# Stick-breaking attention heads: five sample sums, three gate blocks behind the triangles, masks followed bank by bank

## What is computed

```
z = einsum('bqhd,bkhd->bhqk', q, k) * SB_HEAD_DIM ** -0.5
mask = k_pos[None, :] < q_pos[:, None]
log_keep  = where(mask, log_sigmoid(-z), 0)
log_after = cumsum(log_keep, reverse over keys) - log_keep
w = where(mask, exp(log_sigmoid(z) + log_after), 0)
out = einsum('bhqk,bkhd->bqhd', w, v)
```

## Time and profile before

| what | value |
|---|---|
| time, three runs | 4937.35, 4944.21, 4944.24 us; median 4944.21 |
| span of the profiled execution | 4942.6 us (first to last instruction) |
| its own time | not listed apart from the three; the median is 1.6 us above its span |
| TensorE busy | 4694.3 us, 95% of the span |
| heads of attention | from about 67 to 606.7 us, DMA share 0.92, 330 GB/s |
| rest of the program behind them | 4335.9 us, DMA share 0.58 |

### The profile page before, as it was taken

How to read it: one execution, slowest core, us unless ns; L and a number is a source line. 1 busy time by engine, 2 the same in 40 slices (tenths; PEclk the granted TensorE clock), 3 DMA queues, 4 the chain that set the end, 5 groups by cost and what they waited for, 6 DMA issues and landing times. The chain is left out here.

```text
span 4942.6 us, 90862 instructions
## 1 busy us (share of the span) xinstructions
PE 4694.3 (95%) x35332; PEld 4499.6 (91%) x35332; DVE 2965.4 (60%) x4754; ACT 1393.2 (28%) x1798; POOL 2246.3 (45%) x865
## 2 busy tenths in 40 slices
PE   6999989999999898979999989999999999999997
PEld 6999888888888798979998989999999999999997
DVE  3333245555555432339986956655777777777777
ACT  3323322222222221122223333332322322322322
POOL 1222222212221133324443235555877877877876
PEclk8999999999999999989999999998999999999999
DMA  6999833333333277863333455546888888888884
GB/s 237 335 336 337 306 120 132 128 127 129 132 122 131 86 236 245 298 209 104 103 108 154 187 209 186 160 148 240 299 310 300 298 304 299 300 310 299 299 299 170
DMA packets 344271, 1078.94 MB, mean 218 GB/s; under 512 B 99456, under 2 KB 154112, under 8 KB 264960
## 3 DMA queue, kind: packets, MB, share of 16 engines
q1 hardware_dynamic: 292272, 784.66, 45.9%
q0 software_dynamic: 36864, 268.45, 14.5%
q10 hardware_dynamic: 14928, 22.84, 1.3%
HBM read 877.69 MB, written 198.14 MB: 218 GB/s over the span
## 5 line engine op out<-in xcount | busy, mean ns | idle before, releaser
L154 POOL TENSOR_TENSOR wlo<-raw,whi 128x2048 fp32r<-128x2048 f32 x174 | 801.9, 4609 | 2094.6 <-ACT whi L150 1797.9
L168 POOL TENSOR_TENSOR wlo<-raw,whi 128x1024 fp32r<-128x1024 f32 x424 | 1043.2, 2461 | 501.1 <-ACT whi L164 496.4
L164 ACT ACTIVATE whi<-raw 128x1024 fp32r<-128x1024 f32 x424 | 449.6, 1060 | 1012.6 <-PE psS L236 380.3
L236 PE MATMUL accs<-xh,whi 128*128 128x272 f32 x2624 | 577.7, 302 | 54.2 <-POOL wlo L154 26.4
L2234 DVE SCALAR_TENSOR_TENSOR Y<-R,HD,Y 128x2048 f32<-128x2048 f32 x127 | 441.4, 3475 | 233.7 <-DMA R<-in_v,IDX 229.3
L236 PE MATMUL accs<-xh,wlo 128*128 128x272 f32 x2624 | 546.6, 290 | 0.6 <-issue 0.5
L236 PE MATMUL accs<-xl,whi 128*128 128x272 f32 x2624 | 545.4, 289 | 0.0
L236 PE MATMUL accs<-hh,whi 128*128 128x272 f32 (+1 forms) x1696 | 465.1, 323 | 47.4 <-POOL wlo L154 23.1
L236 PEld LDWEIGHTS accs<-xh,whi 128*128 128x128 f32 x2624 | 415.2, 190 | 81.0 <-issue 35.6
L236 PE MATMUL psS<-hh,wlo 128*128 128x416 f32 x1344 | 475.1, 353 | 0.0
L236 PE MATMUL psS<-hh,whi 128*128 128x416 f32 x1344 | 472.2, 351 | 0.0
(11 more groups left out here) (398 smaller groups left out, 9638.4 us busy)
## 6 DMA issues: line engine op xcount, KB each, us to landing
raw<-in_u SPq DMA_DIRECT2D x128, 1024.0 KB, 4.9
raw<-in_v SPq DMA_DIRECT2D x128, 1024.0 KB, 5.7
raw<-in_w_in SPq DMA_DIRECT2D x82, 1024.0 KB, 8.3
at_UI<-in_u SPq DMA_DIRECT2D x64, 1024.0 KB, 9.0
u_d<-at_UO SPq DMA_DIRECT2D x256, 256.0 KB, 6.2
g_d<-STG SPq DMA_DIRECT2D x8, 3328.0 KB, 10.3
Ge<-g_d SPq DMA_DIRECT2D x64, 416.0 KB, 10.8
wo_UI<-in_u SPq DMA_DIRECT2D x24, 1024.0 KB, 8.7
```

The lines of the kernel that those rows point to most:

```text
L154: pool.tensor_tensor(self.lo[:, c % 2, :], self.raw[:, c % 2, :], self.hi[:, c % 2, :].bitcast(F32), ALU.subtract).then_inc(self.split_don ...
L164: act.activation(self.half(self.hi, c, h), self.half(self.raw, c, h), ACT.Copy).then_inc(self.hi_done, 1)
L168: pool.tensor_tensor(self.half(self.lo, c, h), self.half(self.raw, c, h), self.half(self.hi, c, h).bitcast(F32), ALU.subtract).then_inc(se ...
L236: mm = pe.matmul(out, w(k), x(k, n), start=a, stop=z)
```

## The change

The sample's sums take 5 products: one of 160 columns with the triangle, and for each key block b from 1 to 4 one product with the ones that adds it to all earlier blocks at once. Of the gate's 16 blocks 13 stay ahead of the triangles and 3 run behind them. The output products start with blocks 3 and 1 and wait for each mask apart. On ScalarE a small Exp (`at_warm`) loads the table early, and the Sigmoid with the split of weight 5 moves behind the three Exp. On VectorE six turns stand ahead of SPL and two behind the masks. The core of the diff:

```
-        UNITS = 4
+        UNITS, BEHIND = 4, 3
...
-                project(3)
+                pe.wait_ge(S["at_acc_free"], UNITS * i + 4)
+                gate = unit_product(pe, W, 3, acc[1], xh, xl, UNITS, i)
+                for _ in range(KB - BEHIND):
+                    next(gate)
...
-                for b in range(5):
-                    mm = tri(lambda _: zbank["B"][:, 256 + 32 * b:288 + 32 * b], range(b, 5), smp)
+                pe.matmul(zbank["B"][:, 256:416], cst["negtri"][:, :], SPL[:, ZS:ZS + 160], start=False, stop=False,
+                          skip_group_check=True)
+                for b in range(1, 5):
+                    mm = pe.matmul(zbank["B"][:, 256:256 + 32 * b].rearrange("p (c t) -> p c t", c=b), cst["negones"][:, :],
+                                   SPL[:, smp(b)].unsqueeze(1).to_broadcast([P, b, DEC]), start=False, stop=False,
+                                   skip_group_check=True)
                 mm.then_inc(S["tri_ready"], 1)
                 tri(lambda b: z_at(0, b * P), (0, 1, 2, 3), cols).then_inc(S["tri_ready"], 1)
-
+                for mm in gate:
+                    pass
+                mm.then_inc(W.used, 2)
...
-                pe.wait_ge(S["wt_ready"], 4 * i + 4)
...
+                pe.wait_ge(S["wt_ready"], 4 * i + 1)
+                for kb in (3, 1):
+                    outputs(kb)
+                pe.wait_ge(S["wt_ready"], 4 * i + 3)
+                outputs(2)
...
+                pe.wait_ge(S["wt_ready"], 4 * i + 4)
+                outputs(0).then_inc(S["at_o_ready"], 1)
...
-                W.wait_used(act, 3, UNITS, i)
...
-                W.split_hi(act, 5, UNITS, i)
+                act.activation(warm[:, :], warm[:, :], ACT.Exp, scale=0.0).then_inc(S["at_warmed"], 1)
+                act.wait_ge(S["at_warmed"], i + 1)
...
                     act.activation(WT[:, zcols[b]], zbank[b], ACT.Exp).then_inc(S["wt_exp"], 1)
+
+                W.wait_used(act, 3, UNITS, i)
+                act.wait_ge(S["gate_stored"], 16 * i + 16)
+                act.activation(GB[:, :].rearrange("p (h t) -> p h t", h=2), acc[1][:, :, 0:H2],
+                               ACT.Sigmoid).then_inc(S["at_acc_free"], 1)
+                W.split_hi(act, 5, UNITS, i)
...
-                for c in range(TURNS - 1):
+                for c in range(TURNS - 2):
                     R.turn(dve, c, i)
...
-                R.turn(dve, TURNS - 1, i)
-                dve.wait_ge(S["wt_exp"], 3 * i + 3)
...
+                for n, at, parts in ((1, ZCOL[3], 2 * P), (2, ZCOL[2], P), (2, ZS + 128, DEC), (3, ZCOL[0], P)):
+                    dve.wait_ge(S["wt_exp"], 3 * i + n)
...
+                for c in range(TURNS - 2, TURNS):
+                    R.turn(dve, c, i)
```

More of the change, by code:

```diff
@@ L458, in attention @@
         GB, OT = sb("GB", [P, T]), sb("OT", [P, T])
+        warm = sb("at_warm", [P, 1])
         UI, UO = sb("at_UI", [P, 2, D]), sb("at_UO", [P, 2, D])
@@ L531, in head @@
                     pe.wait_ge(S["at_cst"], 64)
-                    pe.wait_ge(S["pad_set"], 1)
+                    pe.wait_ge(S["pad_set"], 2)
                 pe.wait_ge(S["at_acc_free"], UNITS * i + 4)
@@ L567, in head, with outputs @@
                 tri(lambda b: z_at(2, b * P), (2, 3), cols)
-                for b in range(5):
-                    mm = tri(lambda _: zbank["B"][:, 256 + 32 * b:288 + 32 * b], range(b, 5), smp)
+                pe.matmul(zbank["B"][:, 256:416], cst["negtri"][:, :], SPL[:, ZS:ZS + 160], start=False, stop=False,
[4 more added lines that the diff above has]
+                                   skip_group_check=True)
                 mm.then_inc(S["tri_ready"], 1)
                 tri(lambda b: z_at(0, b * P), (0, 1, 2, 3), cols).then_inc(S["tri_ready"], 1)
-                pe.wait_ge(S["vtm_evac"], 2 * i + 2)
-                pe.wait_ge(S["wt_ready"], 4 * i + 4)
-                for kb in range(4):
-                    pe.matmul(psR[:, 1, kb * P:SEQ], VTM[:, kb, :], WT[:, cols(kb)], start=kb == 0, stop=kb == 3,
-                              skip_group_check=True)
+                for mm in gate:
+                    pass
+                mm.then_inc(W.used, 2)
+                def outputs(kb):
+                    return pe.matmul(psR[:, 1, kb * P:SEQ], VTM[:, kb, :], WT[:, cols(kb)], start=kb == 3, stop=kb == 0,
+                                     skip_group_check=True)
+                pe.wait_ge(S["vtm_evac"], 2 * i + 2)
+                pe.wait_ge(S["wt_ready"], 4 * i + 1)
[3 more added lines that the diff above has]
+                outputs(2)
                 for b in range(4):
                     pe.matmul(psS[:, 0, 0:DEC], CV[:, b, :], WT[:, smp(b)], start=b == 0, stop=False)
-                pe.matmul(psS[:, 0, 0:DEC], VTM[0:DEC, 4, :], WT[0:DEC, smp(4)], start=False,
-                          stop=True).then_inc(S["at_o_ready"], 1)
+                pe.matmul(psS[:, 0, 0:DEC], VTM[0:DEC, 4, :], WT[0:DEC, smp(4)], start=False, stop=True)
+                pe.wait_ge(S["wt_ready"], 4 * i + 4)
+                outputs(0).then_inc(S["at_o_ready"], 1)
             head(0, True)
@@ L592, in _ @@
             act.sem_inc(S["o_stored"], 16)
+            act.wait_ge(S["pad_set"], 2)
             with act.Fori(0, HEADS) as i:
@@ L627, in _ @@
                     act.activation(WT[:, zcols[b]], zbank[b], ACT.Exp).then_inc(S["wt_exp"], 1)
+                W.wait_used(act, 3, UNITS, i)
[3 more added lines that the diff above has]
+                W.split_hi(act, 5, UNITS, i)
+                act.wait_ge(S["at_acc_free"], UNITS * i + 6)
+                act.dma_start(gates_d[bass.ds(i, 1)].rearrange("a p n -> (a p) n"), GB[:, :]).then_inc(S["gate_stored"], 16)
                 act.wait_ge(S["at_o_ready"], i + 2)
@@ L642, in _ @@
             dve.memset(KT[:, T:SEQ + P], 0.0).then_inc(S["pad_set"], 1)
+            dve.memset(warm[:, :], 0.0).then_inc(S["pad_set"], 1)
             R.start(dve)
@@ L657, in _ @@
                 ch.end()
-                R.turn(dve, TURNS - 1, i)
-                dve.wait_ge(S["wt_exp"], 3 * i + 3)
-                n = 0
-                for at, parts in ((ZCOL[3], 2 * P), (ZCOL[2], P), (ZCOL[0], P), (ZS + 128, DEC)):
+                for n, at, parts in ((1, ZCOL[3], 2 * P), (2, ZCOL[2], P), (2, ZS + 128, DEC), (3, ZCOL[0], P)):
+                    dve.wait_ge(S["wt_exp"], 3 * i + n)
                     s = slice(at, at + parts)
```

## The result

The changed kernel takes **4984.12 us**, median of 4 runs (4982.93 to 4987.46), against 4943.6 (4 runs, 4937.35 to 4944.24): ratio 1.0085, interval 1.0072 to 1.0098. Slower by 0.85%; forecast 4990 in 4955 to 5010. Its profiled execution has a span of 4981.1 us and a time of 4982.93.

The account below looks back on a forecast made before the run. The prediction saw TensorE and transfers both near their limits, and late weight 4 setting the changed loop. Seven longer loops +47.6, head 0 -7.8, end stores +6 make +46 on 4942.6, so 4988.6; forecast 4990 us, range 4955 to 5010.

Parts of the forecast that it names:

- The loop through weight 4: Mask to mask: moved turns issue weight 4 one round later, ScalarE waits; 73.7 us against 66.9, +47.6 over seven loops.
- landing: Weight 4's load from issue until it has landed: 10.7 us in the loop.
- pace: SP queue, three rounds from a head's first store to the issue of weight 4: 40.5 us.
- The ends: Head 0 ends 7.8 us sooner; at attention's end the wait for the last two turns' stores costs 6 us.
- TensorE's clock: Triangles start at granted clock 0.50 after about 10 us idle; 2.6 us of the loop is slow clock.
- The recurrent branch that follows is otherwise untouched: Behind attention: no further change of time in the recurrent branch.
- TensorE's 5.9 us: Saving per head on TensorE: sample products 2.1, idle time filled by gate blocks 2.2, output products 1.6 us faster.
- GpSimd's part of weight 5 too, with nobody waiting for either sooner: GpSimd's part of weight 5 moves later with the Sigmoid and split, like the gate's store, and this costs nothing.
- transfers speed up: Rival: weight 4 lands in 5.5 us, rounds' loads in 7.1; 62 us a loop, 4908 us; chance 0.13.
- my two theories: Output products' slow clock: it falls behind the idle time ahead of them, or the fifteen narrow products set it off.

Follow-up runs that it names:

- e3: Changed kernel with weight 4's split moved on ScalarE from behind V's copy to behind the Ln: 4933.48 us, ratio 0.9982.
- e4: Changed kernel with weights 3, 4 and 5 loaded one round earlier in SP's list: 4939.07 us, ratio 0.9991.
- e12: Kernel before with ScalarE's new order alone (early Exp, Sigmoid and weight 5's split behind the three Exp), fifteen products: 4930.69 us, ratio 0.9978.
- e8: e1 with all 16 gate blocks ahead of the triangles and one wait for all four masks: 4899.34 us, ratio 0.9913.
- e1: Changed kernel with VectorE's turns back in their old places, everything else still changed: 4898.73 us, ratio 0.9907.
- e5: e1 with all 16 gate blocks ahead of the triangles, output products still following each mask: 4891.35 us, ratio 0.9895.
- e11: Kernel before with five sample products and ScalarE's new order, one wait for all masks: 4908.56 us, ratio 0.9931.
- e9: Kernel before with five sample products in place of fifteen, nothing else: 4945.61 us, ratio 1.0008.
- e7: e1 with one wait for all four masks, gate blocks still behind the triangles: 4892.30 us, ratio 0.9897.
- e2: Kernel before with VectorE's turns alone moved (six ahead of SPL, two behind the masks): 5022.70 us, ratio 1.0150.
- e10: Kernel before with VectorE masking each bank right behind its own Exp, nothing else: 4937.74 us, ratio 0.9991.
- e6: e1 with fifteen sample products of 32 columns in place of the five: 4922.63 us, ratio 0.9964.

## Why the prediction was right, and where it was not

**The loop through weight 4: right, term by term.** Head 1 against the forecast: last mask to first store 121.33 to 123.59, 2.3 (2.35); to the issue of weight 4 at 165.32, 41.7 (40.5); landing, to 176.67, 11.4 (10.7); to the end of the Ln at 184.60, 7.9 (7.9); to the first triangle, 2.9 (2.9); to the last mask at 196.79, 9.3 (9.3). Sum 75.5; the seven loops lie between 71.9 and 75.5, mean 73.7, the forecast's number. That it is hit to the tenth is luck: over the seven loops the mean pace is 41.1 (forecast 40.5), the landing 10.3 (10.7), split to Ln 8.1 (7.9), triangles to last mask 9.0 (9.3), and these misses cancel. That weight 4's is the last of several late loads is shown by e3 and e4, where the loop shrinks by 7.0 and 5.4 and the next one appears.

**The ends: right, one of them by luck.** Head 0 gave 8.5 (7.8), the stores at the end cost 6.3 (6). But the forecast's terms for the stores, 2.35 + 2 x 3.85 + 6.2, add up to 16.25 and not to 15; what was measured is 15.04, because the stores took longer to issue (9.29 us for the eight) and less to land (4.6 us, median). Attention +45.3 against +46.

**TensorE's clock: right.** It is 0.50 behind the wait for SPL, which is 6.2 to 8.1 us long (about 10 forecast); the part ahead of the sample's product took 4.42 us in head 1. In head 3, at full speed by then, the five products took 1.16 (336.68 to 337.84; 1.15 forecast).

**"The recurrent branch that follows is otherwise untouched": 5.4 us off.** From its first to its last weight load of KM (L887, after L908) it takes 918.9 us before and 913.5 after. That is most of the 6.8 us by which the span grows less than the attention, 38.5 against 45.3, and so of the difference between 4990 and 4984. Of the 5.4 us, 3.4 are TensorE's clock (below). That the change did this is not shown: it is one execution of each kernel.

**TensorE's 5.9 us: the amounts right, what brings them in part wrong.** One loop each of before, e12, e8 and e1, without a fall of the clock (length, then TensorE's busy time):

```profile
129.87:195.45 65.58, 63.37 (x475) 60.30 (x475) 22.59 (x22) 22.20 (x24) 18.33 (x4) 1.00 0.95 342
127.96:193.05 65.09, 63.35 (x475) 60.29 (x475) 21.88 (x21) 22.61 (x26) 18.45 (x4) 1.00 0.92 328
184.72:247.00 62.28, 61.17 (x455) 58.10 (x455) 22.16 (x21) 22.50 (x26) 18.45 (x4) 1.00 1.01 364
493.95:554.90 60.95, 60.95 (x457) 58.05 (x456) 22.28 (x21) 22.51 (x25) 18.45 (x4) 1.00 1.00 361
```

From before to e1 the busy time falls by 2.4 us, the idle time from 2.2 to nothing, and slow clock cost 66.9 - 65.6 = 1.3 us of a mean loop before; the forecast had 2.1, 2.2 and 1.6, and a path of 61.0 against 60.95. (The mean loop of e1 is 0.8 longer, mostly for the 4.3 us of waits for SPL in seven loops.) What the forecast had wrong is which edits remove the idle time. It gave all of it to the gate blocks, and nothing to ScalarE's order or to the masks followed apart. The idle time falls with ScalarE's order from 2.2 to 1.74 (e12), with masks apart on VectorE to 1.10 (e8), and to nothing with TensorE's waits apart (e5) or with the gate blocks (e7); either is enough. In mean loops, taken one upon the other: ScalarE's order 1.5, most of it clock (before to e12), five products 2.4 (to e11), masks apart on VectorE 0.6 (to e8), TensorE's waits apart 1.2 (to e5), gate blocks behind **-0.6** (to e1). The step that failed is "GpSimd's part of weight 5 too, with nobody waiting for either sooner": VectorE was held by it for 0.5 us, by a wait that no semaphore shows. The profile of before had the evidence: 1.40 against 0.93 us for the same four masks, in the rows that I divided by four.

**The rival "transfers speed up"** (62 a loop, 4908): its loop is that of e1. But in the changed kernel weight 4's landing stayed at 9.8 to 11.3 us in the seven heads, mean 10.2 (10.7 forecast), though the transfers' share in head 1 fell from 0.94 to 0.86. The 5.5 us that this rival took as the least seen come from a load issued at 608.49, behind the heads; of those issued between 60 and 600 us the least is 8.3, so the trace of before spoke against it more than the forecast said.

## What to carry to other kernels

A piece of filler work that is moved on one engine moves every queue that waits for it: follow the list of the queue, find the critical load behind it, and price it with that load's own place in the list. Two chains that end side by side hide each other's savings: the five products alone gave nothing (e9), ScalarE's order alone 0.2% (e12), both 0.7% (e11), with the clock in a part of each. And when a VectorE instruction with two inputs in SBUF takes longer in some heads than in others, look at what GpSimd runs beside it.

## What the runs showed of the hardware that I had not expected

- **VectorE held by GpSimd.** A mask of 128 columns takes 0.28 us, and up to 4.6 while GpSimd's 4.5 us instruction runs (line 679 in e3: longest 4615 ns, median 286). Scalar_tensor_tensor with two inputs in SBUF is held as tensor_tensor is (e9). No engine's idle time shows it; the instruction counts as busy.
- **The clock elsewhere.** In slices of 2 us, the recurrent branch before has five below 0.98, a loss of 3.4 us (the sum of their missing clock times 2 us); the changed kernel, e1, e4, e7 and e8 have none, and their branches take 913.0 to 913.7 us; e2 has some 18.8 us and a branch of 930.8. One slice of before:

```profile
1016.00:1018.00 2.00, 2.00 (x11) 1.63 (x11) 0.28 (x1) 0.00 (x0) 0.00 (x0) 0.50 1.00 328
```

  Before, 918.9 - 913.5 is 5.4, so 2 us are not explained. Why the clock falls there in some executions is open too; with one profile of each kernel, a cause in the kernel can't be told from chance, and executions of the kernel before differ among themselves by more (4932.58 to 4953.1 us among the 21 measured beside e9 and e10).
- **What sets off the fall of the clock in the heads stays open.** In the kernel before it fell about the end of the 2.21 us of idle time in head 3, but in head 2 already in the fifteen narrow products, with no idle time ahead; so it did in four heads of e6, and not behind the same products in e12 (one head apart). In e9 it fell within 4.39 us of idle time; behind 1.10 (e8) and 1.74 (e11) it did not, and neither did it behind the 2.24 us in head 4 of e10. The us of e10 that holds most of the output products there, then head 2 of the kernel before, in the narrow products:

```profile
400.00:401.00 1.00, 1.00 (x5) 0.71 (x4) 1.00 (x1) 0.00 (x0) 0.00 (x0) 1.00 1.07 451
```

```profile
257.00:258.00 1.00, 1.00 (x11) 1.00 (x10) 0.00 (x0) 0.98 (x3) 0.59 (x1) 0.92 1.01 377
258.00:259.00 1.00, 1.00 (x5) 1.00 (x6) 0.00 (x0) 0.99 (x2) 1.00 (x1) 0.50 1.10 365
```

  Neither of my two theories covers all of these.
